# The modulation rows of a hybrid transformer block: weights as the moving operand, and two of four pieces between slices of the first wave

## The reference, cut to what matters

```python
def adaln(cond, w, b, n):
    m = jax.nn.silu(cond) @ w[:, :n * D_MODEL] + b[:n * D_MODEL]
    return jnp.split(m, n, axis=-1)

h_c = rms_norm(ctx, norm_mix_g[l])
sh_c, sc_c = adaln(c_ctx, w_mod[l], b_mod[l], 2)
p_c = (h_c * (1.0 + sc_c) + sh_c) @ w_in[l][:, K_COL:]
...
sh, sc, g, sh2, sc2, g2 = (m[:, None, :] for m in adaln(c, w_mod[l], b_mod[l], 6))
h = rms_norm(x, norm_mix_g[l]) * (1.0 + sc) + sh
y, _, _ = hybrid_mixer(h @ w_in[l], ...)
```

## Time and profile before

| | |
|---|---|
| median of 3 runs | 1855.27 us (1853.42 to 1855.68) |
| the profiled execution | 1856.96 us, its span 1855.2 us |
| mean granted TensorE clock in it | 0.954 of full |
| TensorE matmuls busy | 1717.6 us (93%) |
| VectorE busy | 1330.5 us (72%) |
| ScalarE busy | 1041.5 us (56%) |
| 16 experts | from 731.4 us on, to near the end |

### The profile page before, as it was taken

The page is one execution under the profiler, slowest core; times in us unless marked ns, Lnnn a source line. Parts: engine busy times, 40 slices in busy tenths (PEclk is TensorE's granted clock), DMA queues, the critical chain, the costliest instruction groups (busy, mean ns, idle before and its releaser), DMA issues.

```text
span 1855.2 us, 21910 instructions
## 1 busy us (share of the span) xinstructions
PE 1717.6 (93%) x8264; PEld 1395.4 (75%) x8272; DVE 1330.5 (72%) x1291; ACT 1041.5 (56%) x955; POOL 146.3 (8%) x137
## 2 busy tenths in 40 slices
PE   6889999999889952999999999999999999999995
PEld 6778998888744432888888888888888888888884
DVE  1147643434833347898998889888889889889897
ACT  4224212234621131777777777777777777777775
POOL 3000210001110000010010010010011011011010
PEclk7589999999989975999999999999999999999998
DMA  9102551121032263999999999999999999999996
GB/s 340 48 2 85 173 176 58 36 71 54 1 104 102 79 227 106 355 369 383 390 370 382 390 371 381 389 372 376 393 372 368 398 373 364 398 382 368 396 378 244
DMA packets 204424, 492.81 MB, mean 266 GB/s; under 512 B 5700, under 2 KB 18792, under 8 KB 204376
## 3 DMA queue, kind: packets, MB, share of 16 engines
q1 hardware_dynamic: 188128, 436.35, 63.3%
q0 software_dynamic: 13248, 47.09, 8.5%
q10 hardware_dynamic: 3000, 8.70, 1.2%
HBM read 471.07 MB, written 21.05 MB: 265 GB/s over the span
## 4 chain that ended last, share of the span: by engine, by line
PE 89%; DVE 7%; ACT 2%; issue 1%; DMA 1%; ACTq 0%; DVEq 0%; POOL 0%; POOLq 0%
PE ps L1003 85%; PE ps L1360 1%; PE ps L1323 1%; PE ps L1021 1%; DVE topi L1777 1%; DVE topv L1776 1%; DVE affT L1779 1%; DVE ring L1860 0%; DVE hs L1679 0%; ACT h2T L901 0%; DVE wl L1827 0%; PE ps L1279 0%; DMA xe<-ffn_in,idx_e 0%; DMA vecs<-in_mlstm_norm_g 0%; DVE hTl L1423 0%
## 5 line engine op out<-in xcount | busy, mean ns | idle before, releaser
L1827 DVE TENSOR_TENSOR wl<-ring,wh 128x2048 fp32r<-128x2048 f32 x384 | 877.8, 2290 | 112.2 <-ACT wh L947 112.0
L947 ACT ACTIVATE wh<-ring 128x2048 fp32r<-128x2048 f32 x384 | 736.9, 1920 | 287.8 <-PE ps L1003 287.8
L1003 PE MATMUL ps<-wh,xel 128*128 128x512 f32 x1024 | 408.6, 399 | 1.4 <-DVE xel L1807 1.4
L1003 PE MATMUL ps<-wh,xeh 128*128 128x512 f32 x1024 | 402.0, 393 | 0.0
L1003 PE MATMUL ps<-wl,xeh 128*128 128x512 f32 x1024 | 401.4, 392 | 0.0
L1003 PEld LDWEIGHTS ps<-wh,xeh 128*128 128x128 f32 x1024 | 192.8, 188 | 45.1
L1003 PEld LDWEIGHTS ps<-wh,xel 128*128 128x128 f32 x1024 | 192.8, 188 | 42.8 <-DVE xel L1807 1.8
L1003 PEld LDWEIGHTS ps<-wl,xeh 128*128 128x128 f32 x1024 | 193.0, 189 | 41.2
L1003 PE MATMUL ps<-wh,hidl 128*128 128x512 f32 x512 | 204.0, 398 | 0.0
L1003 PE MATMUL ps<-wh,hidh 128*128 128x512 f32 x512 | 200.8, 392 | 0.0
L1003 PE MATMUL ps<-wl,hidh 128*128 128x512 f32 x512 | 200.3, 391 | 0.0
(11 more groups left out here) (350 smaller groups left out, 2022.5 us busy)
## 6 DMA issues: line engine op xcount, KB each, us to landing
ring<-in_w_gate_e SPq DMA_DIRECT2D x64, 2048.0 KB, 9.0
ring<-in_w_up_e SPq DMA_DIRECT2D x64, 2048.0 KB, 8.6
ring<-in_w_down_e SPq DMA_DIRECT2D x64, 2048.0 KB, 10.4
mbw<-in_w_mod POOLq DMA_DIRECT2D x32, 512.0 KB, 5.0
hpr<-in_w_in SPq DMA_DIRECT2D x12, 1024.0 KB, 5.5
moda<-in_w_mod SPq DMA_DIRECT2D x4, 2048.0 KB, 18.7
xs<-in_x POOLq DMA_DIRECT2D x8, 512.0 KB, 6.6
ring<-in_w_out SPq DMA_DIRECT2D x2, 2048.0 KB, 7.8
```

Source lines behind the costliest of these rows:

```text
L947: act.activation(whv[m % 4], eview(m), ACT.Copy).then_inc(hi_done, 1)
L1003: return pe.matmul(o, l, r, start=start, stop=stop)
L1827: dve.tensor_tensor(wlv[m % 4], eview(m), whv[m % 4].bitcast(F32), ALU.subtract).then_inc(lo_done, 1)
```

## The change

TensorE makes a piece of the modulation with the operands exchanged (`mod_rows`): `scol` (128x2) is stationary, the weights stream past it 512 columns at a time, eight matmuls in f32 that give a 2x512 row block in bank 6 or 7. VectorE copies it to `mrow` (`mod_copy`), TensorE turns it back into columns with four transposes (`mod_cols`), and VectorE adds the bias as before. The order of the head is now in two lists, one for each of the two engines. Pieces 2 and 3 are used, and piece 3 is made, after the first wave has begun. The splits of the gate weights and of the first half piece move up, on ScalarE into the loop over the tiles, on VectorE before the blocks. The transposes of the spatial weights move behind the wave, and ScalarE's copy of them stands ahead of `hch`.

```diff
+        mrow = at(VTR + 8 * KB, "mrow", [2, MOD_A, W])
...
-        START = "t0 t1 t2 t3 r0 t4 t5 r1 t6 t7 r2 t8 t9 r3".split()
+        HEAD_PE = "t0 t1 t2 t3 r0 t4 t5 c0 r1 t6 t7 t8 t9 c1 r2".split()
+        HEAD_DVE = "t0 t1 t2 t3 t4 t5 r0 t6 t7 c0 t8 r1 t9 c1".split()
...
# ScalarE
             for t in range(NTC + NT):
...
+                if t == 6:
+                    act.wait_ge(gates_in, 8 * 16)
+                    act.activation(wgh[:], wgr[:], ACT.Copy).then_inc(hp_hi, 1)
+                if t == 8:
+                    piece_high(0)
             norm_copy(NTC + NT - 1)
-            act.wait_ge(ws_t, 1)
-            act.activation(wsT[:], ps[:, 5, :].rearrange("p (h q) -> p h q", h=H), ACT.Copy).then_inc(wsT_ready, 1)
...
-            act.wait_ge(gates_in, 8 * 16)
-            act.activation(wgh[:], wgr[:], ACT.Copy).then_inc(hp_hi, 1)
-            piece_high(0)
             for k in range(KT):
                 act.wait_ge(h_mod, k + 1 if k < KT // 2 else k + 1 + KT // 2)
                 act.activation(hTh[:, k], hTr[:, k], ACT.Copy).then_inc(h_hi, 1)
+            act.wait_ge(ws_t, 1)
+            act.activation(wsT[:], ps[:, 6, :].rearrange("p (h q) -> p h q", h=H), ACT.Copy).then_inc(wsT_ready, 1)
             act.wait_ge(h_mod, 2 * KT)
             act.activation(hch[:], hcr[:], ACT.Copy).then_inc(h_hi, 1)
# TensorE
-            def mod_cols(n):
+            def mod_rows(n):
 
                 pe.wait_ge(mod_in[n], 16)
                 pe.wait_ge(scol_ready, 1)
                 if n >= 2:
                     pe.wait_ge(moda_ready, n - 1)
+                for k in range(KT):
+                    last = mm(ps[0:2, 6 + n % 2, :], scol[:, k, :], moda[n][:, k, :], k == 0, k == KT - 1)
+                last.then_inc(moda_done, 1)
+
+            def mod_cols(n):
+
+                pe.wait_ge(moda_c, n + 1)
                 for ct in range(W // P):
-                    for k in range(KT):
-                        last = mm(ps[:, 7 - n % 2, 2 * ct:2 * ct + 2], moda[n][:, k, ct * P:(ct + 1) * P],
-                                  scol[:, k, :], k == 0, k == KT - 1)
-                last.then_inc(moda_done, 1)
-
-            for what in START:
-                {"t": token_tile, "r": mod_cols}[what[0]](int(what[1:]))
-            pe.wait_ge(ws_in, 16)
-            for h in range(H):
-                last = pe.transpose(ps[:, 5, h * P:(h + 1) * P], wsraw[:, h], ident[:])
-            last.then_inc(ws_t, 1)
+                    last = pe.transpose(ps[:, 6 + n % 2, 2 * ct:2 * ct + 2], mrow[0:2, n, ct * P:(ct + 1) * P],
+                                        ident[0:2, 0:2])
+                last.then_inc(moda_t, 1)
+
+            for what in HEAD_PE:
+                {"t": token_tile, "r": mod_rows, "c": mod_cols}[what[0]](int(what[1:]))
...
             pe.wait_ge(hp_lo, 2)
-            pe.wait_ge(wsT_ready, 1)
             for k in range(KT):
                 pe.wait_ge(h_lo, k + 1)
                 for g in range(WAVE):
                     last = mm3(pout(g), *operands(g, k), k == 0, k == KT - 1)
                     if k == KT - 1:
                         last.then_inc(pj_done, 1)
+                if k == 0:
+                    mod_cols(2)
+                    mod_rows(3)
+                if k == 2:
+                    mod_cols(3)
+            pe.wait_ge(ws_in, 16)
+            pe.wait_ge(moda_ready, 4)
+            for h in range(H):
+                last = pe.transpose(ps[:, 6, h * P:(h + 1) * P], wsraw[:, h], ident[:])
+            last.then_inc(ws_t, 1)
             pe.wait_ge(h_lo, KT + 1)
# VectorE
+            def mod_copy(n):
+                dve.wait_ge(moda_done, n + 1)
+                dve.tensor_copy(mrow[0:2, n, :], ps[0:2, 6 + n % 2, :]).then_inc(moda_c, 1)
...
+            for what in HEAD_DVE:
+                {"t": token_norm, "r": mod_copy, "c": mod_bias}[what[0]](int(what[1:]))
+                if what == "t8":
                     dve.wait_ge(hp_hi, 1)
                     dve.tensor_tensor(wgl[:], wgr[:], wgh[:].bitcast(F32), ALU.subtract).then_inc(hp_lo, 1)
+            piece_low(0)
...
+            dve.wait_ge(moda_ready, 2)
+            h_shift(0)
+            h_shift(1)
+            h_low(0)
+            mod_copy(2)
+            h_low(1)
+            h_shift(2)
+            mod_bias(2)
+            h_low(2)
+            h_shift(3)
+            mod_copy(3)
+            h_low(3)
+            for k in range(KT // 2):
+                hc_shift(k)
+            mod_bias(3)
+            dve.wait_ge(moda_ready, 4)
+            h_shift(4)
+            for k in range(KT // 2 + 1, KT):
+                h_shift(k)
+                h_low(k - 1)
+            h_low(KT - 1)
+            for k in range(KT // 2, KT):
+                hc_shift(k)
```

More of the change, by code:

```diff
@@ L290, in hybrid_block @@
         moda_done = sem("moda_done")
+        moda_c = sem("moda_c")
+        moda_t = sem("moda_t")
         moda_ready = sem("moda_ready")
@@ L690, in norm_copy, with piece_high @@
                 act.activation(dst, two(b, b + 2).rearrange("p (k t) -> p k t", k=KT), ACT.Copy).then_inc(xt_free, 1)
+            def piece_high(i):
+                act.wait_ge(hp_in[i % 2], 16 * (i // 2 + 1))
+                act.activation(hph[i % 2][:], hpr[i % 2][:], ACT.Copy).then_inc(hp_hi, 1)
             for t in range(NTC + NT):
@@ L700, in _ @@
                     norm_copy(t - 1)
-            norm_copy(NTC + NT - 1)
-            act.wait_ge(ws_t, 1)
-            act.activation(wsT[:], ps[:, 5, :].rearrange("p (h q) -> p h q", h=H), ACT.Copy).then_inc(wsT_ready, 1)
-            def piece_high(i):
-                act.wait_ge(hp_in[i % 2], 16 * (i // 2 + 1))
-                act.activation(hph[i % 2][:], hpr[i % 2][:], ACT.Copy).then_inc(hp_hi, 1)
-            act.wait_ge(gates_in, 8 * 16)
-            act.activation(wgh[:], wgr[:], ACT.Copy).then_inc(hp_hi, 1)
-            piece_high(0)
+                if t == 6:
[3 more added lines that the diff above has]
+                    piece_high(0)
+            norm_copy(NTC + NT - 1)
             for k in range(KT):
@@ L1097, in chain_ends @@
                 pe.wait_ge(row_dve, 2)
+                pe.wait_ge(wsT_ready, 1)
                 pe.transpose(ps[0:1, 6, 0:R64], mxc[:, 0:1], ident[0:R64, 0:R64])
@@ L1388, in mod_bias @@
                 bias = vcol[:, VROW["b_mod"] + a:VROW["b_mod"] + a + nc4].unsqueeze(2).to_broadcast([P, nc4, 2])
-                dve.wait_ge(moda_done, n + 1)
+                dve.wait_ge(moda_t, n + 1)
                 link(dve.tensor_tensor(mod[:, a:a + nc4, :],
-                                       ps[:, 7 - n % 2, 0:2 * nc4].rearrange("p (j c) -> p j c", c=2),
+                                       ps[:, 6 + n % 2, 0:2 * nc4].rearrange("p (j c) -> p j c", c=2),
                                        bias, ALU.add))
@@ L1411, in _, with h_shift @@
             dve.tensor_reduce(selc[:], sred[:].rearrange("p (z d) c -> p d c z", z=2), AX.X, ALU.add)
-            for what in START:
-                {"t": token_norm, "r": mod_bias}[what[0]](int(what[1:]))
-                if what == "t9":
+            for what in HEAD_DVE:
+                {"t": token_norm, "r": mod_copy, "c": mod_bias}[what[0]](int(what[1:]))
+                if what == "t8":
                     dve.wait_ge(hp_hi, 1)
                     dve.tensor_tensor(wgl[:], wgr[:], wgh[:].bitcast(F32), ALU.subtract).then_inc(hp_lo, 1)
+            piece_low(0)
             dve.wait_ge(xt_free, NTC + NT)
+            def h_shift(k):
+                dve.tensor_scalar(hTr[:, k], hTr[:, k], amix[:, k, 0:1], mod[:, k, 0:1],
+                                  ALU.mult, ALU.add).then_inc(h_mod, 1)
             def h_low(k):
@@ L1423, in h_low, with hc_shift @@
                 dve.tensor_tensor(hTl[:, k], hTr[:, k], hTh[:, k].bitcast(F32), ALU.subtract).then_inc(h_lo, 1)
[L1425 to L1438, removed]
+            def hc_shift(k):
+                dve.tensor_scalar(hcr[:, k], hcr[:, k], amix[:, k, 1:2], mod[:, k, 1:2],
+                                  ALU.mult, ALU.add).then_inc(h_mod, 1)
+            dve.wait_ge(moda_ready, 2)
[21 more added lines that the diff above has]
+                hc_shift(k)
             dve.wait_ge(h_hi, KT + 1)
```

## The result

| | before | with the change |
|---|---|---|
| median of four runs each | 1855.47 us | 1826.59 us (1822.42 to 1828.81) |
| ratio, 95% interval | | 0.9842 (0.983 to 0.9854) |
| the profiled execution | 1856.96 us | 1822.42 us, its span 1820.6 |
| mean granted TensorE clock | 0.954 | 0.973 |

What follows compares the result with a forecast made beforehand. The head was taken as bound by TensorE's four modulation pieces at a low clock, then a 13.7 us wait for `hpl`. Terms -41.2 + 7.7 - 2.4 + 0.2 + 5.8 + 0.6 + 1.8 = -27.5 gave 1827.8 us, range 1820 to 1834.

Steps and rivals of the forecast that it cites:

- Equal matmul time, another clock: Modulation pieces: exchanged operands save no matmul time at an equal clock but lift it, 6.9 us a piece against 13.7 at half.
- B: Rival: two stationary columns don't count as work for the clock, pieces stay at 13.7 us; gain 1.4, 1853.9 us; chance 0.10.
- C: Rival: f32 matmuls with a narrow stationary side don't overlap, 1.02 us each; 9.2 us slower, 1864.5; chance 0.04.
- A: Rival: the clock lifts only in part; piece 2, the first slice and part of piece 3 low; +8, 1836 us; chance 0.11.
- Piece 0: First modulation piece on TensorE: starts at 22.66 at the low clock, 6.9 us plus 0.7 for the lift, ends at 30.2.
- Tiles 8 and 9: Last tiles of the head: ScalarE is the bound, `hph` costs 1.90 us there, TensorE idles 3 to 6 us.
- Piece 2: Third modulation piece: starts low at 50.6, costs 1.4 us more, ends at 58.9; the wave starts at 59.0, 41.2 us earlier.
- Inside the wave: Between the wave's slices: piece 3 and the turns add 7.7 us, a warm start takes 2.4, VectorE's turn adds 0.2.
- Behind the wave: After the wave TensorE waits for `wsT`, `hch` and `hcl` before the next group: +5.8 us, nothing before.
- The clock's dip: After the wave, 5 us of idle TensorE may cost the clock; a new lift costs 0 to 2.4 us, taken as 1.8.
- the row work's lag: After the wave, the first gate copies queue behind `wsT` on ScalarE, so row work and convolutions lag: +0.6 us.
- The far stages: Low clock stretches in the 13th to 16th slices fall otherwise against the work, worth 3 us either way.

Runs made afterwards that it cites:

- Rows only: The kernel before with the pieces made as rows and turned back, everything else in the old order; 1831.76 us, ratio to before 0.9876.
- order only: The changed kernel with pieces made the old way (weights stationary, two columns streaming), without row copies or turns back; 1848.38 us, ratio to before 0.9961.
- moving 128: The changed kernel with each piece in 32 matmuls of 128 moving columns in place of 8 of 512; 1825.60 us, ratio to before 0.9836.
- hph back: The changed kernel with ScalarE's split `hph` moved back behind the last tile's copy; 1824.26 us, ratio to before 0.9829.
- piece 3 ahead: The changed kernel with piece 3 made right after piece 2, before the wave, its turn back staying behind the third slice; 1825.47 us, ratio to before 0.9832.
- copy first: The changed kernel with VectorE's copy of piece 0's rows ahead of the scaling of tiles 4 and 5; 1827.19 us, one run.
- piece 2 in the gap: The changed kernel with piece 2 before tiles 8 and 9, while TensorE waits for ScalarE, and piece 3 before the wave; 1818.23 us, ratio to before 0.9805.

## Why the prediction was right

The forecast was 1827.8 and the median is 1826.59, within the range. In the profiled execution the terms of its sum come to -30.0 for -27.5 (31.3 up to group 6, less 1.3 behind it), the far stages not counted. Its steps, one by one:

- **Equal matmul time, another clock.** Right. Rows only gave 23 us with pieces of 7.0 to 7.9, order only kept 13.65 where the clock stayed at 0.50. At an equal clock the two forms are alike by these runs too: the old one has 13.65 x 0.50 = 6.8 us in piece 0 and 9.70 x 0.72 = 7.0 in piece 3 of order only, the new one 7.03 at 1.00. The rows at 551 us that the 0.43 was read from have the clock at 1.00 too (551.0 to 554.5). Rivals B and C fall: no piece of 13.7 at 0.50, and 16 records in 6.96 us, where eight matmuls at C's 1.02 would take 8.2, so matmuls with two stationary columns do overlap. C's isolated pair of 1.02 us is two steps of 0.43 and a drain of 0.16, by which eight records are longer (3.60) than the step to the next group (3.44). Of A only the low start of piece 2 came (0.82, 1.5 us longer than the others), which the forecast itself had at 1.4; the first slice (58.0 to 62.6) and piece 3 were at 1.00. A's price was added up wrong: 5.5 and 2.4 + 2 make 9.9 and 1838, not 8 and 1836.
- **Piece 0** was forecast to end at 30.2 and ended at 29.35. The premise that TensorE is at the low clock when piece 0 begins didn't hold in this execution, so the 0.7 for a late lift was not needed. That is luck: in the other nine traces with 512-column rows piece 0 took 7.5 to 8.3 us, 0.5 to 1.2 more than 7.03.
- **Tiles 8 and 9** wait for ScalarE. Right, 5.6 us in two waits. Tile 9 came at 47.10 for 48.3; `hph` was charged 1.9 and measured 1.5.
- **Piece 2** was to run from 50.6 to 58.9, and the wave to start at 59.0: 49.52, and 58.00.
- **Inside the wave**, +7.7 for piece 3 and the turns, -2.4 for a warm start: from the wave's start to its end it took 40.9 us for 35.4 before, 5.5 more as forecast. The 0.2 for VectorE at piece 3's columns can't be seen in it, no wait stands there.
- **Behind the wave**, +5.8: TensorE resumes 5.4 us after the wave's end at 98.9. The clock's dip was taken at 1.8 and the row work's lag at 0.6. From group 6 to the mLSTM it took 304.2 us before; 305.5 in the change's profiled execution, and 306.8 to 308.2 in the traces of order only, moving 128, hph back, piece 3 ahead, copy first and piece 2 in the gap, which all have that wait; 304.2 to 304.5 in the four with it removed or shortened. So 2.4 was a fair size for both together. But most of it is the dip: in the change the clock is at 0.50 for the first 2.9 us [the window from 104.30], and half of that, 1.45, is about the 1.3 lost; in hph back it is so for 6 us from group 6 on, and half of that is 3.0 for 2.8 lost. The lag of the row work, 0.6, doesn't show in these two.
- **Order only** is close to rival B, which was taken at 1.4 us of gain; it measured 6.6. That the rival did not come true hid this. The failing steps are small ones in a row: piece 1 began at 39.5 for 40.8, piece 2 at 61.1 for 63.4, piece 3 ended at 90.0 for 94.4, and group 6 began at 126.3 for 131.8. A part of it is no error of the rival's: it counts the copies and the turns back, which this run doesn't have. The rest was priced too near the low clock: the wave's first slice at 6.4 (5.7 measured), piece 3 at some 10.5 (9.7).
- **The far stages.** They were given 3 us either way for the low stretches of the clock; in the profiled execution they gave 4.6. From mLSTM to experts the traces have 289.0 to 292.2 us with the same instructions, and the execution shown of before has the longest.

That the clock rises on transposes shows not only in the row at 42 us. In the change's trace TensorE had done nothing but transposes before piece 0:

```profile
18.49 1.97 PE L1026 MATMUL ps<-ident,xs 128*128 128x128 f32 x8 [1.76 <-DVE xs L1398]
20.77 1.62 PE L1026 MATMUL ps<-ident,xs 128*128 128x128 f32 x8 [0.30 <-DVE xs L1398]
22.32 7.03 PE L1008 MATMUL ps<-moda,scol 128*2 128x512 f32 x16
```

Tile 2's eight transposes have the low-clock length (1.97 us, as tile 9's at 0.50), tile 3's 1.62 are between that and the 1.09 us of tile 8, and piece 0 has its full-clock length (7.03). So the lift came during tile 3. The granted clock of the windows can't be used there: it stands at 1.00 from the start of each trace to its first change, also where sixteen transposes took 3.68 us. Transposes don't always lift it, though: before the change the sixteen from 53.04 on (3.67 us) left it at 0.50 all through piece 2 (56.5 to 70.1). Piece 2's lift in the new trace came after transposes and matmuls in a row, so it decides nothing. On gaps: after 4.8 us of waiting the clock was at 0.50 [the window from 104.30], after the 2.0 us wait for `gf` the matmuls soon had their full-clock length (0.36, then 0.28 from the second on, at 1.00). But a short wait is no safe one by these rows: in the change tile 8 has the full-clock length (1.09 us) after 2.59 us and tile 9 the low one (1.97) after another 2.99, and in the run with the spatial weights in the gap and `hph` back the clock fell inside tile 8, after a wait of 2.15 us (1.52 us for tile 8, 0.50 from 45.0 on, 1.97 for tile 9).

## What to carry to other kernels

In a product with two rows, choose the operand order by the clock and not only by the matmul time at an equal clock: that was the same here, but with the wide matrix as the moving operand a piece ran at 1.00 in 7.03 us, and with it as the stationary operand at 0.50 in 13.65. When a block is moved behind a stage, look at what stands after it in the queue of every engine that serves it: the transposes of the spatial weights behind the wave, with their 0.6 us copy ahead of `hch` in ScalarE's list, cost 5 to 6.5 us against the run that has both in the gap. And look first for the time in which the engine itself waits for another: two blocks of TensorE work put where it waited for ScalarE gave some 14 us, and placing piece 3 between slices of a stage that had no gap gave nothing.

## What the runs showed of the hardware that was not expected

Cutting the rows into 32 matmuls of 128 columns cost next to nothing (7.15 us a piece for 7.03) and kept the clock (1.00). Two stationary columns are enough to keep it: 16 records, with 1.30 us of weight loads in 7.00 us, held it at 1.00 [the window from 62.60]. And the total of one program moved by 6.4 us from run to run (1822.42 to 1828.81), more than several of the edits here are worth. The mean granted clock of these two runs was 0.973 and 0.970, so clock dips are the likely cause; only one of the four has a trace, so that isn't shown. This is why the small edits are read from places in the trace.
